# One region for everything between the two attentions of a hybrid MLA/NSA trunk: the order of the work written out by hand, without barriers

## What is computed

```python
# end of mla_mixer
o = o.reshape(B, S, MLA_HEADS * MLA_V) * jax.nn.silu(z)
return o @ w_out                       # (512 x 2048) @ (2048 x 1024), added to x
# front of nsa_mixer, with h = rms_norm(x, norm_g[1])
q, kc, vc, ks, vs, kw, vw, gl, z = jnp.split(h @ w_in, splits, axis=-1)
q = rope(rms_norm(q.reshape(B, S, NSA_HEADS, DK), g_q), pos, NSA_ROT)
ks = rope(rms_norm(ks.reshape(B, S, G, DK), g_k[1]), pos, NSA_ROT)
kw = rope(rms_norm(kw.reshape(B, S, G, DK), g_k[2]), pos, NSA_ROT)
gates = jax.nn.sigmoid(gl).reshape(B, S, NSA_HEADS, 3)
# 31 windows of 32 tokens, stride 16
k_cmp = compress(kc.reshape(B, S, G, DK), tok_idx, pe_k, w1_k, w2_k)
k_cmp = rope(rms_norm(k_cmp, g_k[0]), pos[:, cmp_end], NSA_ROT)
v_cmp = compress(vc.reshape(B, S, G, DV), tok_idx, pe_v, w1_v, w2_v)

def compress(t, tok_idx, pe, w1, w2):
    blk = t[:, tok_idx] + pe[:, None, :]
    blk = jnp.moveaxis(blk, 3, 2).reshape(B, n, G, L * d)
    return jax.nn.silu(blk @ w1) @ w2
```

## Time and profile before

| what | value |
| --- | --- |
| median of 3 runs | 1158.87 us (1158.2 to 1162.5) |
| the profiled execution, its own time | 1157.0 us |
| its span, first to last instruction | 1155.2 us |
| TensorE busy | 1054.9 us, 91% |
| DVE, ACT, POOL busy | 470.9, 425.8, 414.8 us |
| mean granted clock of TensorE | 0.950 |

### The profile page before, as it was taken

One profiled execution on the slowest core, in us unless ns is written; L12 is line 12 of the kernel. 1 busy time (PEld: TensorE's weight loads), 2 busy tenths in 40 slices (PEclk: granted clock), 3 DMA queues, 4 the chain that ended last, 5 costly groups with the idle time before them and its releaser, 6 DMA issues. The chain is left out here.

```text
span 1155.2 us, 17907 instructions
## 1 busy us (share of the span) xinstructions
PE 1054.9 (91%) x6487; PEld 912.3 (79%) x6487; DVE 470.9 (41%) x1269; ACT 425.8 (37%) x1124; POOL 414.8 (36%) x566
## 2 busy tenths in 40 slices
PE   6999989999999978995999998998499899999888
PEld 6888788898899866775778887886478787788776
DVE  5140156666666551003001104437656554555421
ACT  5333365555555451114111111112344444444320
POOL 2534275555545413433434435417311111111131
PEclk9999999999999998998999999679598999988999
DMA  5422211011010004230332234101000000000021
GB/s 188 136 83 73 88 47 40 21 40 40 20 40 20 2 1 135 84 109 2 109 106 80 95 108 117 40 17 37 5 1 1 1 0 0 0 0 0 1 91 54
DMA packets 42344, 58.67 MB, mean 51 GB/s; under 512 B 8725, under 2 KB 25386, under 8 KB 42282
## 3 DMA queue, kind: packets, MB, share of 16 engines
q1 hardware_dynamic: 40672, 57.42, 15.7%
q10 hardware_dynamic: 1610, 0.43, 0.2%
HBM read 55.62 MB, written 2.10 MB: 50 GB/s over the span
## 5 line engine op out<-in xcount | busy, mean ns | idle before, releaser
L157 POOL TENSOR_TENSOR w_lo<-w_raw,w_hi 128x2048 fp32r<-128x2048 f32 (+1 forms) x30 | 136.7, 4558 | 239.9 <-ACT w_hi L151 239.9
L89 PE MATMUL bank<-w_hi,h_hi 128*128 128x512 f32 (+2 forms) x480 | 189.9, 396 | 8.0 <-PEq L1019 3.1
L90 PE MATMUL bank<-w_lo,h_hi 128*128 128x512 f32 (+2 forms) x480 | 186.2, 388 | 0.0
L91 PE MATMUL bank<-w_hi,h_lo 128*128 128x512 f32 (+2 forms) x480 | 186.0, 388 | 0.0
L151 ACT ACTIVATE w_hi<-w_raw 128x2048 fp32r<-128x2048 f32 (+1 forms) x30 | 56.9, 1897 | 252.3 <-PE bank L246 200.8
L1526 ACT ACTIVATE prob<-bank,negmax 128x128 f32<-128x128 f32 (+3 forms) x128 | 67.5, 527 | 142.4 <-DVE negmax L1592 142.3
L89 PEld LDWEIGHTS bank<-w_hi,h_hi 128*128 128x128 f32 x480 | 92.5, 193 | 25.9 <-issue 4.5
L1475 PE MATMUL bank<-kv,probT 128*128 (+1 forms) x640 | 94.0, 280 | 13.9 <-ACT probT L1536 11.5
L1592 DVE TENSOR_REDUCE negmax<-bank 128x1 f32<-128x128 f32 (+3 forms) x128 | 61.8, 489 | 108.8 <-PE bank L1447 107.1
L1475 PEld LDWEIGHTS bank<-kv,probT 128*128 128x128 f32 x640 | 87.4, 200 | 23.7 <-ACT probT L1536 20.9
L91 PEld LDWEIGHTS bank<-w_hi,h_lo 128*128 128x128 f32 x480 | 92.0, 192 | 17.8
(11 more groups left out here) (248 smaller groups left out, 2372.3 us busy)
## 6 DMA issues: line engine op xcount, KB each, us to landing
w_raw<-in_nsa_w_in SPq DMA_DIRECT2D x10, 1024.0 KB, 5.0
w_raw<-in_mla_w_in SPq DMA_DIRECT2D x8, 1024.0 KB, 5.2
w_raw<-in_mla_w_out SPq DMA_DIRECT2D x8, 1024.0 KB, 5.2
w_raw<-in_nsa_w_in SPq DMA_DIRECT2D x8, 984.0 KB, 5.0
w_raw<-in_mla_w_uq SPq DMA_DIRECT2D x16, 288.0 KB, 3.1
w_raw<-in_mla_w_ukv SPq DMA_DIRECT2D x16, 256.0 KB, 3.4
w_raw<-in_nsa_w_out SPq DMA_DIRECT2D x4, 1024.0 KB, 5.1
w_raw<-in_mla_w_in SPq DMA_DIRECT2D x4, 704.0 KB, 5.3
```

The costliest lines, as they stand in the source:

```text
L89: nc.tensor.matmul(out, a[0], b[0], start=start, stop=False)
L90: nc.tensor.matmul(out, a[0], b[1], start=False, stop=False)
L91: return nc.tensor.matmul(out, a[1], b[0], start=False, stop=stop)
L157: nc.gpsimd.tensor_tensor(w_lo[slot][:, :, 0:width], w_raw[slot][:, :, 0:width], w_hi[slot][:, :, 0:width].bitcast(F32), ALU.subtract).the ...
```

## The change

The regions 1 to 6 above are gone; their work is appended to the first region, on each engine in an order that is written out, and all waits are on semaphores that count single steps. Memory is laid out by hand in one slab.

- `mid` lists the 26 pieces of weights: 8 of w_out, then w_in in the order k, v and gates (4 chunks of 492 columns), q (3 chunks), z (2 chunks). The buffers of a piece are freed by the count of finished products `m_done`; the small matmul after each piece is gone. The first piece's split is done at the end of head 14, the second's at the end of head 15.
- o is turned set by set: sets 0 and 1 inside head 15, sets 2 and 3 after it, each later one after the products of an earlier k tile (`out_products`, whose first four pieces go over k tiles first and token tiles second).
- x is turned without its norm. The left half is turned in w_out's sixth piece, the right half in the first piece of w_in. The factor of the norm is applied by ACT when a bank leaves (`leave`, ACT instead of DVE).
- The bias of the compression is the 129th column of the hidden layer's matmuls: the position embedding stands behind kc and vc in `ctk` and `ctv`. The 32 matmuls are split into 8 parts of 4, one after each token tile (`hidden_part`).
- The compressed k is made for all four groups on 128 partitions, with one second-layer matmul, and counts as an item of one head. Therefore the positions of the windows are loaded four times (`pos_i`), 3 DMAs more on ACT's queue.
- The items (25: 4 of ks, 4 of kw, the compressed k, 16 of q) follow a table that gives the squares a place between ACT's splits and exits, and the factors a place after POOL's splits. The turns of ks and kw are two rows of `beside`, in the second and third chunk of q.
- On SP's queue pe, w2, w1k and w1v stand behind the third piece of w_in.

```diff
+                OUT_PIECES, OUT_J = 8, 4
+                KV_CHUNKS, KV_W = 4, (2 * CVW + CVW + GW) // 4
+                mid = [(mla_w_out[0], j * KP, c * CW, CW) for c in range(2) for j in range(OUT_J)]
+                in_cols = ([(QW + c * KV_W, KV_W) for c in range(KV_CHUNKS)] + [(c * CW, CW) for c in range(QW // CW)]
+                           + [(QW + KV_CHUNKS * KV_W + c * CW, CW) for c in range(Z1 // CW)])
+                mid += [(nsa_w_in[0], j * KP, c0, width) for c0, width in in_cols for j in range(2)]
+                NM, NIN = len(mid), len(in_cols)
...
+                        if g == OUT_PIECES + 2:
+                            sp.wait_ge(m_done, NT * OUT_PIECES)
...
+                            sp.dma_start(w1k[:, :, :], nsa_w1_k[0].rearrange("(l d) e -> d l e", d=DK)).then_inc(w1k_in, 16)
+                            sp.dma_start(w1v[:, :, :], nsa_w1_v[0].rearrange("(l d) e -> d l e", d=DV)).then_inc(w1v_in, 16)
...
+                        if h == H - 1:
+                            turn_o(0)
                         values(h, 2)
+                        if h == H - 1:
+                            turn_o(1)
...
+                    def out_products():
+                        for g in range(OUT_J):
+                            pe.wait_ge(m_lo, g + 1)
+                            for k in range(KP):
+                                kt = g * KP + k
+                                pe.wait_ge(o_lo_made, kt + 1)
+                                for t in range(NT):
+                                    if kt == 0 and t == NT - 1:
+                                        pe.wait_ge(o_free, 4 * H + 1)
+                                    last = mid_product(g, t, k, o_hi, o_lo)
+                                    if k == KP - 1:
+                                        last.then_inc(m_done, 1)
+                                if kt + 4 < ZZ // P:
...
+                                last.then_inc(m_done, 1)
+                                if g == OUT_J + 1:
+                                    turn_x1(t)
...
+                        for l in range(4 * part, 4 * part + 4):
+                            last = nc.tensor.matmul(bank[b][0:d, 0:G * NC + 1], w[:, l, :],
+                                                    ct[:, l:l + G * SEQ + 1:STRIDE], start=l == 0, stop=l == LCMP - 1)
...
+                    beside = {(0, 0, 1): lambda: [turn_x1(k) for k in range(4, 8)], (0, 1, 1): turn_pe,
+                              (4, 0, 1): second_k, (4, 0, 3): second_v, (6, 1, 1): turn_k_cmp}
+                    for g in range(G):
+                        beside[(1, (g + 1) // 4, (g + 1) % 4)] = lambda g=g: turn_kc(g)
+                        beside[(5, 0, g)] = lambda g=g: turn_k(0, g)
+                        beside[(6, 0, g)] = lambda g=g: turn_k(1, g)
+                    for part in range(8):
+                        vc = {1: 0, 2: 1, 3: 2, 5: 3}.get(part)
+                        beside[(2, part // 4, part % 4)] = (
+                            lambda part=part, vc=vc: [hidden_k(part)] + ([turn_vc(vc)] if vc is not None else []))
+                        beside[(3, part // 4, part % 4)] = lambda part=part: hidden_v(part)
...
+                            for j in range(2):
+                                g = OUT_PIECES + 2 * c + j
+                                pe.wait_ge(m_lo, g + 1)
+                                for t in range(NT):
+                                    if j == 0 and c == 0:
+                                        pe.wait_ge(x1_left, NT + t + 1)
+                                    elif j == 0:
+                                        pe.wait_ge(n_left, NT * (c - 1) + t + 1)
+                                    for k in range(KP):
+                                        if c == 0 and t == 0:
+                                            pe.wait_ge(h1_lo_made, j * KP + k + 1)
+                                        last = mid_product(g, t, k, h1_hi, h1_lo)
+                                    last.then_inc(m_done, 1)
+                                    if (c, j, t) in beside:
+                                        beside[(c, j, t)]()
 
...
-                    act.dma_start(pos_i[0:NCMP, NT:NT + 1],
-                                  positions[0, LCMP - 1:SEQ].rearrange("(n s) -> n s", n=1).rearrange("n s -> s n")
-                                  [0:SEQ - LCMP + 1:STRIDE, :]).then_inc(pos_loaded, 16)
+                    for g in range(G):
+                        act.dma_start(pos_i[g * NC:g * NC + NCMP, NT:NT + 1],
+                                      positions[0, LCMP - 1:SEQ].rearrange("(n s) -> n s", n=1).rearrange("n s -> s n")
+                                      [0:SEQ - LCMP + 1:STRIDE, :]).then_inc(pos_loaded, 16)
...
+                        if h >= H - 2:
+                            mid_high(h - H + 2)
...
+                        for dst, d0, s0, s1 in parts[c]:
+                            last = nc.scalar.activation(dst[:, t, d0:d0 + s1 - s0], bank[t][:, s0:s1],
+                                                        ACT.Silu if c >= 7 else ACT.Copy, scale=r)
+                        last.then_inc(n_left, 1)
...
+                                 9: [lambda: square1(6), lambda: square1(7), lambda: square1(8)],
+                                 10: [lambda: square1(9), lambda: square1(10)] + [lambda u=u: k_high(u) for u in range(4)],
...
+                        for s in range(2 * NIN):
+                            todo = tasks.get(s, [])
+                            if 1 <= s <= 2 * NIN - 2:
+                                mid_high(OUT_PIECES + 1 + s)
...
+                            if s % 2 == 0:
+                                for do in todo:
+                                    do()
+                            else:
+                                for t in range(NT):
+                                    if s == 1 and t == 0:
+                                        act.wait_ge(r1_made, 1)
+                                    leave(s // 2, t)
+                                    if t < len(todo):
+                                        todo[t]()
...
+                        if s <= 2 * NIN - 2:
+                            mid_low(OUT_PIECES + 1 + s)
+                        for n in factors_at.get(s, ()):
+                            factor_item(n)
```

781 lines of the change are left out of this document (418 added, 363 removed).

## The result

The changed kernel takes 1097.29 us (median of 4 runs, 1095.9 to 1098.05); the kernel before took 1160.4 beside it (4 runs, 1158.2 to 1162.5). The ratio is 0.9455, with a 95% interval of 0.9431 to 0.9479. I had said 1092.3, with 1080 to 1109 as the range. The saving was put at 66.6 us and is 63.1 beside the kernel before. The direction, the size and the mechanism were right. What was off is in two small terms at the edges.

What follows compares the result with a forecast made beforehand. TensorE, busy 91%, bounds the kernel, with time to be had between the attentions. From the profiled 1157.0, less 66.5 there, plus 1.4 at the start, less 1.5 in the second attention: 1090.4, as median 1092.3 us; range 1080 to 1109.

Steps and rivals of the forecast that it cites:

- The middle: From the first attention's last product to the second attention's first transposes: 337.7 us instead of 404.2, 66.5 us less.
- Joint one: From the last head to the output projection's first product: some 1.5 us, where it took 13.2.
- joint two: From the last product to the second attention's transposes: 1.7 us, made of ACT's last Silu 0.85 and 0.87.
- The 16 parts of the hidden layers: Compression: 28.5 us for matmuls with the bias column, plus 0.1 for each break between products, 1.6.
- The 13 small instructions of the second layers, pe and kcmp: Compression: at most a transpose's 0.125 us each, with three breaks, 1.9 us in all.
- The start: Before ACT's first split: three more position DMA issues at 0.45 us each delay the first product; 1.4 us more.
- The second attention: Its first 10 us: with less idleness ahead the clock may hold, 0 to 4.3 us less; taken as 1.5 less.
- Rival 1: Hidden layer's chunks: the clock falls inside them, +15 us, 1107 us; chance 0.15.
- Rival 2: From chunk 4 on: norms run late, TensorE waits at several pieces, +15 us, 1107 us; chance 0.10.
- Rival 3: Compression: hidden layer's matmuls cost 0.14 us instead of 0.222 among products, 10.5 us less, 1082 us; chance 0.07.
- Rival 4: ACT's queue: squares, norms and splits wait in a ring, 7.5 us over eleven pieces, 82, 1174 us; chance 0.02.
- Rival 5: Joints: some wait of the new order holds TensorE as the barrier did, +12 us, 1104 us; chance 0.04.

Runs made afterwards that it cites:

- e4: Changed kernel with each hidden layer of the compression in one piece at its chunk's end, instead of 8 parts between products; 1095.37 us, ratio 0.943.
- e7: Changed kernel with the compression's bias made by one-column matmuls ahead of the hidden layers, whose matmuls go back to 128 columns; 1110.12 us, one run.
- e2: Changed kernel with one load of 128 window positions in place of four loads of 31, for timing only; 1085.71 us, one run.
- e6: Changed kernel with ScalarE making the high part of each weight piece from the third on four times over; 1114.55 us, one run.
- e9: Changed kernel with the three additional position loads after ScalarE's second split, plus identity transposes at the second attention; 1089.68 us, ratio 0.9379.

## Why the prediction was right, point by point

**The middle, 337.7 against 336.9.** Most of its terms held one by one. Joint one was put at 1.5 from the old end of the head, 0.3 of it for turn_o(0) inside the head; that set took 0.44, which the table counts with the start, and the rest 1.2, so 1.64 in all; a set between products 0.43 and 0.43 (0.35 from the set at 434.41 to the next product, and 0.08 more on that product); a piece of 512 columns 11.16 and 11.15; the row of 16 transposes of x 2.0 and 1.7; the hidden layer's matmul 0.222 and 0.219; joint two 1.7 and 1.57. The 16 parts of the hidden layers were put at 28.5 + 1.6 = 30.1 and measure about the same (13.8 for k's eight, 16.3 for v's), but not as reasoned: breaks cost nothing in k and 0.3 in v, where I had put 0.1 for each, so the agreement of the sum is partly luck. The 13 small instructions of the second layers, pe and kcmp were put at 1.9 with their breaks; up to the next product they take 0.9, and 0.3 more stands on the products behind the second layers. The products go without a wait and at the full clock, which the sum took for granted by pricing every one at the earlier trace rows: before, the same stretch was granted 0.91 on average. e4 and e7 show a part of what that rested on: with unbroken layers or rows of one-column matmuls put back, the clock falls under the compression again. How much of the many falls before (a clock of 0.79 over 88 us) came from the waits there instead, no run shows.

**The start, +1.4 against +5.96.** The step that failed is the price of three more DMA issues, "one for positions takes 0.45", with 2.2 as the upper end. They cost 4.84. The row was of the right kind and from the wrong moment: an issue before some 3.6 us is cheap, and those behind it ran into waits of 2.5 and 3.3 us. The profile before had a sign of it that I read as an end of the range, not as a mechanism: the gains, further down the same list, one of them a single issue of 2.16 us at 4.19:

```profile
4.19 2.16 ACTq L650 DMA_DIRECT2D gk<-in_mla_g_k  x1
```

Another 0.44 is turn_o(0) in the last head, for which I had put 0.3 in joint one. The 0.7 left over is the difference between the changed kernel and e2 after their first products, which goes with the low clock of the changed kernel's start; one trace each, in a stretch that varied by over 5 us among twelve, doesn't show it.

**The second attention, -1.5 against +1.65.** The step's reasoning, that a shorter idle time ahead would let the clock hold, wasn't borne out by the trace: it fell all the same, to 0.50 for over 10 us. Over the twelve traces of the code after, the mean is 324.9, 1.8 under the one trace of before, near to the 1.5; but with a spread of 6 us between traces neither is shown. The total carries this luck too: with a second attention of 322, as other executions of the same code had, the profiled time would have been 6 us nearer to the forecast.

**The rivals.** Rival 1 exists, is worth 2.7 us and not 15, and doesn't occur in this change (e4). Rival 2 didn't come about. Rival 3 didn't: 0.219 in place of 0.14. Rival 4's ring doesn't close even with 5.76 us more in each piece (e6). Rival 5 didn't: both joints closed to within 0.2 of the sum.

**The best version** of those run is e9, 1089.68 us, 6.8 under the changed kernel. The part of it that traces show is one edit, the additional loads taken out of the list of issues ahead of the first split: 4.84 us at the first product, and some 0.6 of that returned as a longer wait for w_lo.

## What to carry to other kernels

A long dense stretch was predicted to a microsecond in 337 from a handful of rows, with misses of about a microsecond in single terms, which in part cancelled: price the products by their spacing where nothing disturbs them, the insertions by the spacing across one, and then count waits. What went wrong was at the edges, where a few microseconds hang on one queue or on the clock's luck: a DMA issue is to be priced by the issues that stand around it at that moment, and three small loads in front of the first work cost more here than 16 cuts in the middle. And of two kernels one trace each isn't enough to price something of 6 us; the same code gave 322 and 328 in the second attention and 410 and 416 in the first. Where a stretch repeats to the tenth, as the middle does, read the experiment there.
